# Two fused blocks on one core: block 1's v is turned a second time, and the difference is added back

## The reference

```python
xn = rms_norm(h, mix_norm[l])
proj = jnp.einsum("bsd,dp->bsp", xn, w_in[l]) + b_in[l]
q, k, v, cb, cc, cx, ga, gc = jnp.split(proj, splits, axis=-1)
attn = sliding_window_attention(q, k, v, sinks[l])
conv = cb * causal_depthwise_conv(cc * cx, conv_w[l])
```

## Time and profile before

| what | value |
|---|---|
| median of 2 runs | 1216.84 us |
| the profiled execution | 1217.13 us |
| its span in the trace | 1215.0 us |
| PE busy | 1202.1 us (99%) |
| DVE busy | 827.8 us (68%) |
| ACT busy | 553.6 us (46%) |
| POOL busy | 385.8 us (32%) |
| DMA queue of the weights | 116.28 MB, 29.6% of the 16 DMA engines' time |

### The profile page before, as it was taken

The page is one execution under the profiler, slowest core; times in us unless marked ns, Lnnn a source line. Parts: engine busy times, 40 slices in busy tenths (PEclk is TensorE's granted clock), DMA queues, the critical chain, the costliest instruction groups (busy, mean ns, idle before and its releaser), DMA issues.

```text
span 1215.0 us, 15012 instructions
## 1 busy us (share of the span) xinstructions
PE 1202.1 (99%) x5822; PEld 1012.2 (83%) x5822; DVE 827.8 (68%) x1520; ACT 553.6 (46%) x954; POOL 385.8 (32%) x283
## 2 busy tenths in 40 slices
PE   9999999999999999999999999999999999999997
PEld 7888888888888888888888879898888889898886
DVE  5868735466888537653569877767967866677864
ACT  6557533324444324433334566653335555643433
POOL 0035279997000000000003238775203033464200
PEclk9999999999999999999999999999999999999999
DMA  8232232322323232233223333222223332222221
GB/s 303 75 101 70 70 114 87 104 78 95 104 87 119 90 99 89 90 112 96 93 73 96 121 112 95 89 88 78 78 72 101 105 105 88 87 90 95 76 70 70
DMA packets 35911, 117.42 MB, mean 97 GB/s; under 512 B 3968, under 2 KB 4480, under 8 KB 35840
## 3 DMA queue, kind: packets, MB, share of 16 engines
q1 hardware_dynamic: 35552, 116.28, 29.6%
q10 hardware_dynamic: 288, 0.18, 0.0%
HBM read 114.35 MB, written 2.10 MB: 96 GB/s over the span
## 4 chain that ended last, share of the span: by engine, by line
PE 87%; DVE 7%; ACT 3%; issue 1%; POOL 1%; DMA 0%; SPq 0%; ACTq 0%; DVEq 0%
PE ps L284 84%; DVE RA L261 3%; DVE FA L273 2%; ACT RA L253 2%; PE ps L1415 1%; DVE FA L261 1%; POOL RA L261 1%; DVE RA L273 1%; PE ps L813 1%; ACT RA L257 1%; DMA FA<-w_units 0%; PE ps L479 0%; ACT FA L257 0%; PE ps L521 0%; POOL FA L261 0%
## 5 line engine op out<-in xcount | busy, mean ns | idle before, releaser
L284 PE MATMUL ps<-RA 128*128 128x512 f32 (+1 forms) x5470 | 1179.3, 376 | 6.4 <-DVE RA L261 4.1
L284 PEld LDWEIGHTS ps<-RA 128*128 128x128 f32 x5470 | 974.3, 189 | 188.9 <-DVE RA L261 4.8
L253 ACT ACTIVATE RA<-FA 128x1024 fp32r<-128x1024 f32 (+4 forms) x337 | 279.7, 857 | 338.7 <-PE ps L284 165.2
L261 DVE TENSOR_TENSOR RA<-FA,RA 128x1024 fp32r<-128x1024 f32 (+6 forms) x302 | 322.3, 1078 | 161.7 <-ACT RA L253 157.5
L261 POOL TENSOR_TENSOR FA<-FA 128x512 f32<-128x512 f32 (+1 forms) x88 | 116.4, 1324 | 443.3 <-ACT FA L257 417.3
L277 POOL TENSOR_SCALAR FA<-FA 128x256 f32<-128x256 f32 (+3 forms) x117 | 147.2, 1270 | 161.9 <-DVE FA L281 160.8
L273 DVE SCALAR_TENSOR_TENSOR FA<-ps,FA 128x512 f32<-128x512 f32 (+3 forms) x137 | 98.1, 721 | 90.2 <-PE ps L284 44.9
L261 POOL TENSOR_TENSOR RA<-FA,RA 128x512 fp32r<-128x512 f32 (+1 forms) x37 | 70.4, 1914 | 111.2 <-ACT RA L253 111.2
L258 ACT ACTIVATE FA<-FA 128x512 f32<-128x512 f32 (+4 forms) x109 | 60.3, 555 | 97.1 <-DVE FA L1385 76.0
L273 DVE SCALAR_TENSOR_TENSOR FA<-FA 128x4 f32<-128x4 f32 (+4 forms) x166 | 84.4, 515 | 20.6 <-ACT FA L253 7.9
L257 ACT ACTIVATE FA<-ps,FA 128x512 f32<-128x512 f32 x56 | 38.1, 684 | 108.3 <-PE ps L284 108.3
(11 more groups left out here) (43 smaller groups left out, 274.9 us busy)
## 6 DMA issues: line engine op xcount, KB each, us to landing
FA<-w_units SPq DMA_DIRECT2D x189, 512.0 KB, 3.5
FA<-rel SPq DMA_DIRECT2D x16, 256.0 KB, 3.2
FA<-w_units SPq DMA_DIRECT2D x8, 384.0 KB, 3.0
FA<-x SPq DMA_DIRECT2D x8, 256.0 KB, 5.7
FA<-x_rows SPq DMA_DIRECT2D x4, 512.0 KB, 9.2
FA<-dmat SPq DMA_DIRECT2D x8, 256.0 KB, 3.3
out<-FA SPq DMA_DIRECT2D x8, 256.0 KB, 2.2
FA<-w_units SPq DMA_DIRECT2D x2, 256.0 KB, 4.2
```

Source lines behind the costliest of these rows:

```text
L253: return lambda eng: eng.activation(dst, src, ACT.Copy)
L261: return lambda eng: eng.tensor_tensor(dst, a, b, op)
L284: return lambda e: e.matmul(dst, a, b, start=start, stop=stop_)
```

## The change

In slot 0, ACT makes a copy of the identity in the rounded type (`identr`, into IDR), and SP copies VF to another place, VM, that is read as the rounded type (`vm`, a DMA from SBUF to SBUF of 128x512, 256 KB). PE turns VM with IDR into bank 6 (`vU`, four turns that wait for `vm` and `identr`). ACT takes bank 6 to a temporary (`vc`), DVE subtracts bank 7 from it (`vd`), multiplies the difference by 2^20 and adds bank 7 (`vs`). The pair `vh`, `vl` is then made from the temporary rather than from bank 7. If both turns give the same bits the difference is zero and v is what it was.

```diff
+VM, IDR = Z + 26368, Z + 26880
...
                 gemm_tall(key, b, xh, xl, 8, (lambda k: [f"x0.l{k}"]) if slot == 0 else None)
                 if slot == 0:
+                    A("identr", ["ident"], copy(R(IDR, 128), F(ID, 128)))
+                    dma("vm", ["vf"], Rf(VM), F(VF), "vm")
                     for i in range(4):
                         T("vT" if i == 3 else None, ["vf"] + take("bank7") if i == 0 else [],
                           lambda e, i=i: e.transpose(bank(7, 128, 128 * i), F(VF + 128 * i, 128), F(ID, 128)))
...
                 if slot == 0:
-                    src, dh, dl = stacked_v("v", 7, VV, [])
-                    A("vh", ["vT"], copy(dh, src))
+                    for i in range(4):
+                        T("vU" if i == 3 else None, ["vm", "identr"] + take("bank6") if i == 0 else [],
+                          lambda e, i=i: e.transpose(bank(6, 128, 128 * i).bitcast(F32R), R(VM + 128 * i, 128), R(IDR, 128)))
+                    tv, tvn = t_slot()
+                    A("vc", ["vU"] + take(tvn), copy(F(tv), bank(6)))
+                    free("bank6", "vc")
+                    V("vd", ["vc", "vT"], sub(F(tv), F(tv), bank(7)))
+                    V("vs", ["vd"], stt(F(tv), F(tv), float(2 ** 20), bank(7), ALU.mult, ALU.add))
+                    _, dh, dl = stacked_v("v", 7, VV, [])
+                    src = F(tv).rearrange("p (h d) -> p h d", h=8)
+                    A("vh", ["vs"], copy(dh, src))
                     V("vl", ["vh"], sub(dl, src, dh.bitcast(F32)))
-                    free("bank7", "vl")
+                    free("bank7", "vs")
+                    free(tvn, "vl")
                 a_slot(slot, evacuate)
```

## The result

The changed kernel takes 1225.62 us (median of 2 runs, 1225.17 and 1226.08) against 1216.84 us: 1.0073 times as long, with a 95% interval of 1.0056 to 1.0089. That is slower, clear of the noise, and by less than 2%. It lies inside the range, 1.0 us above the forecast of 1224.6, on the side that was forecast. The profiled execution takes 1225.17 us, with a span of 1223.3 us where it was 1215.0.

What follows compares the result with a forecast made beforehand. The prediction took TensorE (PE), busy 99% of the span, to bound the kernel. It added a 5.7 us shift from waiting for the copy and 2.1 us for a fallen clock to 1216.84, giving 1224.6 us, range 1221.6 to 1226.7.

Steps and rivals of the forecast that it cites:

- The bound and the place: PE, busy 99% of the span, has no slack; a wait put into its queue after unit cc0 moves everything behind it.
- The copy's issue: On SP, the copy queues behind the load of unit 15, issued at 69.60, and so is issued at 69.97.
- The copy's landing: The copy lands 3.8 us after its issue, at 73.77; bounds from 72.17 to 74.3.
- the pair at 800 us: A weight load and a 256 KB transfer behind it, issued 0.37 us apart, landing after 3.5 and 3.8 us.
- The turns: PE's four new turns, ahead of the scores of stage 0, take 4 x 0.14 = 0.56 us.
- The shift: The load for stage 0's first score on PE moves from 68.66 to 74.33, 5.7 us; bounds 4.1 to 6.2.
- The clock: PE's clock falls to 1.2 GHz in the wait for the copy, costing 2.1 us, bounds 0 to 4.2; chance 0.52.
- the row of the end: At the kernel's end the granted clock fell to 0.50 some 5.1 us after PE's last product.
- The work costed at nothing: New ACT and DVE work between PE's turns and `vl`, 2.0 us, is covered by unit cx0 and costs nothing.
- The clock does not fall: Rival: PE waits for the copy as said but its clock stays, 1222.5 us; chance 0.34.
- Early landing: Rival: the copy lands at 72.17, the shift is 4.1 us, the clock stays, 1220.9 us; chance 0.07.
- The time comes back: Rival: later PE waits, before 137 or around 254, absorb the shift, 1216.8 to 1218 us; chance 0.03.

Runs made afterwards that it cites:

- e1: Changed kernel with the copy of v put into SP's queue earlier, ahead of the load of unit 15 and behind that of unit 14; 1217.06 us.
- e2: Changed kernel with the copy left in place, but the four new turns and the work behind them moved from slot 0 to slot 1; 1217.12 us.
- e9: Changed kernel with a transfer of the same size from HBM in the copy's place, the new turns reading rounded x; 1224.81 us.
- e5: Changed kernel with the copy issued from the same place in the code, but on ACT's own DMA queue instead of SP's; 1217.31 us.
- e10: Changed kernel with the copy and the load of unit 15 exchanged on SP, both still waiting for the same subtraction; 1223.23 us.
- e0: The changed kernel run once more, nothing altered; 1225.05 us, 1.0067 times the kernel before.
- e3: Changed kernel with 20 unread products of 512 columns on PE between the old turns and the new ones; 1222.22 us.
- e7: Changed kernel with 10 unread products on PE between the old turns and the new ones; 1224.96 us.
- e8: Changed kernel with 15 unread products on PE between the old turns and the new ones; 1223.81 us, runs from 1222.25 to 1225.60.
- e6: Changed kernel with the copy put behind the load of unit 16 on SP, so two loads stand ahead of it; 1227.95 us.

## Why the prediction was right, point by point

*The bound and the place.* No slack on PE: right. A wait put into PE's queue moved everything behind it, and taking the wait away (e1, e2) took the loss away with the added work still in place.

*The copy's issue.* 69.97 was worked out, 70.00 it was, behind the load of unit 15 as the order on SP had it.

*The copy's landing.* 3.8 us was taken, 4.35 it was: this term of the sum was 0.55 us too small, and the measured value lies just above the upper bound (4.3). The step that failed is the choice of the pair at 800 us "since size, queue and the load ahead are the same and only the source differs". The source counted: e9, the same place with the source in HBM, gave 3.70. What the pair did get right is that the load ahead decides: without one, 2.3 us (e5, e10), 0.1 above the lower bound that I had taken from the writes to memory. The Trainium skill, page "DMA: Bandwidth & Descriptors", section "Anatomy of one DMA — SWDGE (gpsimd) path", gives a formula for another path, by which 256 KB take 2.6 us, an estimate. For the copy with nothing ahead the trace agrees to 0.3 us; the section counts no queue, and the queue was 2 us of it here.

*The turns.* 0.56 us was taken; their loads took 74.89 - 74.39 = 0.50 us at the lower clock. In e1's chain, at the higher clock, the four cost 0.29 us.

*The shift.* 5.7 us forecast, 6.21 measured, all of the difference from the landing.

*The clock.* It fell, the likeliest case. Its price, 2.1 us by the kernel's first products, was 2.1 in the profile of the changed kernel and 3.2 in that of e0, and 2.8 us by the medians of e0 and e3. The size is right, but in part by luck: the price went by how long PE worked at the lower level, some 5 us in the changed kernel and some 7 in e0, and nothing tied that to the slow stretch at the kernel's start. The reasoning to the chance of a fall was wrong. I took the 5.1 us at the kernel's end for something that a wait has to reach, and called 3.2 us "too short for the fall by the row of the end". In the changed kernel it fell 3.5 us after PE's last work (69.0 to 72.5), in e0 after 2.3, and e10 and e7 lost it in waits of 3.1 and 3.3 us. The chance of a fall should have been well above 0.52, and a pause longer than 5.1 us, which tipped me to it, was not what it took. The Trainium skill, page "TensorE: Matmul & The Clock Gate", section "HAM oscillation — how this bites in real kernels", names waits on DMAs between bursts of products as what brings the lower rate back, and was the better guide here. The trace agrees, with 0.50 from 72.5 to 79.4.

*The work costed at nothing.* Right: the masks of stage 0 ended 0.6 us later than worked out, which is the copy's 0.55 us, and the cover of unit cx0 held. The slower products at the lower clock widened it: stage 1's scores came at about 83.5, where 81.0 was worked out without a fall.

*The rivals.* "The clock does not fall" is what e3 makes: 1222.22 us for the forecast of 1222.5. Early landing is e10, but with a fall: 1223.23 us for 1220.9. "The time comes back" did not happen in the changed kernel, where the 8.34 us of the chain stand in the span. In e3 half a microsecond did come back, at the place "around 254" that this rival named (below). The sum, 5.7 + 2.1 = 7.8 us, stands against 6.2 + 2.1 = 8.3 in the profile.

## What to carry to other kernels

Before a DMA that an engine will wait for is put into a queue, look at what stands ahead of it there and what that waits for: its data had long been ready, and it still came late, because it stood behind a prefetch that waited for a free buffer. A consumer on the bounding engine belongs behind work that is long enough to cover the transfer; either moving the issue by one place, ahead of that prefetch (e1), or the consumer by one unit (e2) gave the whole 8 us back. On TensorE a wait is to be priced with its clock: 5.4 us of waiting cost 8, and the 1.9 us wait of e8 cost up to 3.4 us on top of itself.

## What the runs showed of the hardware that was not expected

**The clock's fall has no fixed distance to the last product.** After PE's last work it fell after 5.1 us at the end of the kernel before, 3.5 us in the changed kernel's wait, 2.3 in that of e0 (e7's expectation gives 3.5 for both profiles, which is wrong for this one), 3.3 in e7, 2.4 in e9, about 1.3 in e6 (stretch from 70 to 71, 0.51, with PE's last work before 68.8) and 1.0 in e10. In e8 it fell 1.3 us after PE had resumed. It stayed low for 3.4 us in e8, for 6.8 us in the changed kernel, for 10.2 in e0, and longest in e6, 13.7 us, where most of the 7.9 us of waiting lay in it. The rows below are those of e6.

```profile
68.80:70.00 1.20, 0.00 (x0) 0.00 (x0) 1.09 (x2) 0.66 (x1) 0.00 (x0) 1.00 0.00 0
70.00:71.00 1.00, 0.00 (x0) 0.00 (x0) 0.72 (x1) 0.00 (x0) 0.00 (x0) 0.51 0.45 123
```

**A copy within SBUF and a load ahead of it in the same queue both took longer.** Each took 0.6 us more than in the pair with both sources in HBM (e9). By what means was not tried.

**ACT issued a DMA ahead of activations that stand before it in ACT's code.** In e5 the issue stood behind `identr` in ACT's queue and happened some 2 us before `identr` ran. So the place of a call in the code, which stands above as its place in the engine's queue, did not set when this DMA was issued. That was seen in this one kernel, and what sets the lead was not tried.

**A little time came back in some profiles.** In e3 the piece of 64 starts 5.6 us late, but the median lies only 5.2 us above that of before. In the profile of before, subtractions on DVE interrupt PE's chain at 252.45; the changed kernel and e0 have the same interruption some 8 to 9 us later. In e3 the chain runs through, as it does in e6, e7, e8 and e10. The same stretch of the chain takes 258.70 + 48.62 - 137.25 = 170.07 us before and 169.57 in e3, half a microsecond less. First the kernel before, then e3:

```profile
137.25 115.20 PE ps L284 x508
...
258.70 48.62 PE ps L284 x213
```

```profile
142.96 169.57 PE ps L285 x748
```

Why that interruption is there in some profiles and not in others was not settled. All kernels but the changed one were profiled once, so whether it goes with the kernel or with the execution is open too. The differences above between e0 and e3 or e6 can carry this half microsecond.
